# Scaling the attention probabilities on GpSimd in a two-layer hybrid decoder step

## Chip, cores and metric

One Trainium2 chip, one of its cores. The metric is the device time of the whole program in microseconds; a lower time is better. The kernel computes one inference step of two trunk layers for 512 prompt tokens with 16 learned tokens ahead of them, and for 8 sample tokens, with the same weights: 536 columns in all.

## The reference, cut to what matters

Each layer runs an attention over chosen keys, a gated linear recurrence, a merge of the two, and a feed-forward part. The change is in the prompt's attention: scores, softmax, and the product with the values.

```python
def attend_selected(q, k_sel, v_sel, valid):
    ...
    s = jnp.einsum('btngd,btknd->btngk', qg, k_sel.astype(jnp.float32)) * (HEAD_DIM ** -0.5)
    s = jnp.where(valid[:, :, None, None, :], s, -jnp.inf)
    p = jax.nn.softmax(s, axis=-1)
    o = jnp.einsum('btngk,btknd->btngd', p, v_sel.astype(jnp.float32))
    ...
def mixer_back(x, att, rec_o, gates, g_rec, w_pa_l, w_pb_l, w_o_l):
    ...
    a = att @ w_pa_l
    b = rec.reshape(B, T, REC_V) @ w_pb_l
    return x + (jax.nn.sigmoid(ga) * a + jax.nn.sigmoid(gb) * b) @ w_o_l
```

The softmax is over 528 keys or fewer for a tile of 128 queries. Its last step, dividing each row by its sum, is the operation that moves.

## The kernel before, in words

All orders of work are written out by hand, one instruction list for each engine, with semaphores between them. A layer has a front part (projections with the indexer and the top-k beside them), an **attention stage**, a merge, an output projection and the feed-forward part. Weights come in by DMA as tiles `raw`; ScalarE rounds each to a high part `w_hi` (`split`, L1426), GpSimd takes the remainder `w_lo` = `raw` - `w_hi` (`rest`, L667), and TensorE multiplies with both (L809). There are two buffers of `w_hi` and of `w_lo`, so the split of weight unit n waits until unit n-2 has been multiplied.

The attention stage has 17 blocks a layer (`BLK`), in the order (head pair 0: tiles 0, 1, 2, the short last tile of all heads, 3), then head pairs 1 to 3 with tiles 0 to 3. This text numbers them 0 to 16. A block has two halves s (two heads), and tile j has 128, 256, 384 or 512 key columns; block 3, the short tile, has 528. For each half of a block:

1. TensorE makes the scores in PSUM (`qk`, L1105), one block ahead.
2. VectorE adds the mask and takes the row's extremum, and writes `E` (`att_scores`, L2447); it waits also for the turns of the block before, since `E` is one buffer.
3. ScalarE takes the exponential of `E` in place, with the row's sum beside it (`att_exps`, L1695).
4. VectorE takes the reciprocal of both halves' sums in one instruction (L2456, semaphore `recips`).
5. ScalarE multiplies `E` by the reciprocal in place (`att_probs`, L1703, semaphore `probs`).
6. TensorE transposes `E` into PSUM (`turn`, L772), ScalarE copies it out as `pT` (L1709, L1712), TensorE multiplies it with the values (`pv`, L1137), and ScalarE copies the result out (L1609).

Between these steps stands the recurrence's work, put there by tables (`DVE_AHEAD`, `DVE_BEHIND`, `ACT_AHEAD`, `PE_AMID` and so on, with the block as key). On VectorE it is above all the steps `diff` (L2355, L2357) and `product` (L2364, L2366): `tensor_tensor` instructions with both inputs in SBUF, of 1024 or 1056 elements in each of 128 partitions. `DVE_BEHIND` is what stands right behind the reciprocal of a block:

```python
DVE_BEHIND = {..., 2: [("diff", 0, 1), ("diagonal", 1)],
              3: [("product", 0, 0), ("product", 0, 1)], 4: [("diff", 2, 0), ("scores", 0, 0)],
              5: [("product", 1, 0), ("product", 1, 1)], 6: [("product", 2, 0), ("product", 2, 1), ("scores", 1, 0)],
              7: [("diff", 4, 0), ("scores", 2, 0)], 8: [("product", 3, 0), ("product", 3, 1)],
              9: [("product", 4, 0), ("product", 4, 1), ("scores", 3, 0)], 10: [("diff", 6, 0), ("scores", 4, 0)],
              11: [("product", 5, 0), ("product", 5, 1)], 12: [("product", 6, 0), ("product", 6, 1), ("scores", 5, 0)],
              ..., 14: [("v_blk", 0)], ...}
```

`diagonal` and `scores` there are predicated copies out of PSUM (L2318, L2336), `v_blk` is a `tensor_tensor` of 8 partitions with both inputs in SBUF (L2387).

GpSimd clears two tensors ahead of the stage (L747, L750), takes the first two remainders of the merge's weights at its start, and then waits for the third, whose high part ScalarE makes behind the stage (`split_merge(2)`).

Of the kernel before, what the change touches and what calls it, by code (L numbers as in the profile page):

```python
# [76 lines left out]
def build(nc, t, out):  # L77
# [7 lines left out]
    ACT, ALU, AX = mybir.ActivationFunctionType, mybir.AluOpType, mybir.AxisListType  # L85
# [17 lines left out]
    WIDTH = [128, 256, 384, 512, 528]  # L103
# [7 lines left out]
    UA, UB, UC, UP, UO = 0, 16, 32, 48, 64  # L111
# [30 lines left out]
    BLOCKS = 17  # L142
# [9 lines left out]
    BLK = [(0, 0), (0, 1), (0, 2), (0, 4), (0, 3)] + [(n2, j) for n2 in range(1, 4) for j in range(4)]  # L152
# [44 lines left out]
    with ctx:  # L197
        def sb(name, shape, dt=f32):
            return ctx.enter_context(nc.sbuf_tensor(name, shape, dt))
# [52 lines left out]
        row_st = sb("row_st", [P, 2, 4])  # L252
# [7 lines left out]
        def place(name, shape, offset, dt=f32):  # L260

            n = 1
            for d in shape[1:]:
                n *= d
            n *= 1 if dt == u8 else 4
            assert offset + n <= size, (name, offset + n, size)
            return nc.alloc_sbuf_tensor_at(name, shape, dt, offset=base + offset)
# [30 lines left out]
        E = place("E", [P, 2, TP], o_ss)  # L298
# [93 lines left out]
        def wait(eng, name, L, per, n):  # L392

            eng.wait_ge(S[name], L * per + n)

        def hold(eng):

            eng.sem_inc(S["held"], 1)
# [27 lines left out]
        def turn_tile_of(s):  # L426

            return work[0][:, 512 * s:512 * s + 512]

        def last_turn(s):  # L430

            return acc[s][0:16, 1, 0:128]

        def short_turned(s):

            return pT[:, s, :, :].rearrange("p c t -> p (c t)")
# [53 lines left out]
        block = ctx.enter_context(nc.Block())  # L490
# [168 lines left out]
        def _(pool):  # L659
            pool.wait_ge(S["par_ready"], 1)  # L660
            for L in range(DEPTH):
                def rest(u, slot, kt):


                    s = slot % 2
                    pool.wait_ge(hi_done, L * UNITS + u + 5)  # L666
                    pool.tensor_tensor(w_lo[s][:, 0:kt, :], raw[slot][:, 0:kt, :], w_hi[s][:, 0:kt, :].bitcast(f32),  # L667
                                       ALU.subtract).then_inc(lo_done, 1)
# [79 lines left out]
                wait_unit(pool, L, UC + 15)  # L748
                hold(pool)
                pool.memset(Atail[:, :, :], 0.0).then_inc(S["scores_cleared"], 1)  # L750
                with pool.Fori(0, 4) as g:
                    for i in range(4):
                        rest(UP + g * 4 + i, i, 4)
                with pool.Fori(0, 2) as g:
# [628 lines left out]
        def _(act):  # L1383
# [26 lines left out]
            for L in range(DEPTH):  # L1410
# [115 lines left out]
                for j in range(1, 5):  # L1526
                    n = TILES[j][1]
                    for h in range(8):
# [3 lines left out]
                        w = min(512, WIDTH[j])  # L1532
# [165 lines left out]
                def att_probs(block):  # L1698

                    j, w = BLK[block][1], WIDTH[BLK[block][1]]  # L1700
                    for s in range(2):
                        wait(act, "recips", L, BLOCKS, block + 1)
                        act.activation(E[:, s, 0:w], E[:, s, 0:w], ACT.Copy, scale=row_st[:, s, 3:4])\  # L1703
                            .then_inc(S["probs"], 1)
                    for s in range(2):
                        act.wait_ge(turn_filled[s], L * BLOCKS + block + 1)
                        ps = turn_tile_of(s)
                        if j < 4:
                            act.activation(pT[:, s, 0:j + 1, :], ps[:, 0:(j + 1) * P].rearrange("p (c t) -> p c t", t=P),  # L1709
                                           ACT.Copy).then_inc(turn_drained[s], 1)  # L1710
                        else:
                            so(act.activation(short_turned(s)[:, 0:256].rearrange("p (m t) -> p m t", t=16),  # L1712
                                              ps.rearrange("p (m t) -> p m t", t=32)[:, :, 0:16], ACT.Copy))
                            act.activation(short_turned(s)[0:16, 256:320].rearrange("p (m t) -> p m t", t=16),
                                           last_turn(s).rearrange("p (m t) -> p m t", t=32)[:, :, 0:16],
                                           ACT.Copy).then_inc(turn_drained[s], 1)

                for block in range(STEPS):
                    if block < BLOCKS:
                        att_exps(block)  # L1720
                    if 0 < block <= BLOCKS:
                        att_drain(block - 1)
                    rec_steps(ACT_AHEAD.get(block, ()))
                    if block < BLOCKS:
                        att_probs(block)
                    rec_steps(ACT_BEHIND.get(block, ()))
# [874 lines left out]
```

## Time and profile before

| | |
|---|---|
| time, median of 3 runs | 2178.01 us (2175.06 to 2178.32) |
| the profiled execution's own time | 2177.8 us |
| its span in the trace | 2175.9 us |
| mean granted TensorE clock | 0.966 of full speed |
| busy TensorE, VectorE, ScalarE, GpSimd | 2009.2, 1210.8, 784.9, 760.8 us |
| attention stages, from the first `qk` to the first merge unit | 443.0 to 577.7 us and 1497.8 to 1635.2 us |

The span is measured from the first to the last instruction of the trace, and the time of the execution lies 1.9 us above it. Busy time is an average over all stages; in a stage it can be quite another engine that the rest waits for, so the stages are looked at one by one. A row of the timeline gives the start, the duration, engine, line, operation, output and inputs, and in brackets how long the engine had stood idle and for whom.

### The profile page before, as it was taken

How to read it: one execution, taken by the hardware profiler on the slowest of the kernel's cores; microseconds unless marked ns; L12 is line 12 of the kernel's file. 1: busy time of each engine (PE TensorE's matmuls, PEld its weight loads, DVE VectorE, ACT ScalarE, POOL GpSimd, SP SyncE). 2: the span in 40 equal slices, each digit the busy share in tenths (PEclk: the TensorE clock that was granted, in tenths of full speed). 3: DMA queues.
4: the chain of work that ended last, by engine and by line, in shares of the span. 5: the costliest groups of instructions: out<-in, count | busy, mean ns of one | idle time of the engine just before them, and what ended most of it. 6: DMA issues, size and time to landing. Idle time of an engine off the chain costs nothing. (4 is left out here: it accounts for less than half of the span.)

```text
span 2175.9 us, 40128 instructions
## 1 busy us (share of the span) xinstructions
PE 2009.2 (92%) x15610; PEld 1906.0 (88%) x15610; DVE 1210.8 (56%) x2159; ACT 784.9 (36%) x1217; POOL 760.8 (35%) x414
## 2 busy tenths in 40 slices
PE   3998999877989999999999899988888899999998
PEld 2987899866779999999999889987667899999998
DVE  3286777687465543045346677886754564412433
ACT  3243323267233343222323342225752334322233
POOL 1642338200034343443455223641001444434333
PEclk9999999899989999999999999998997999999999
DMA  5312236111332222332241323431033322223322
GB/s 132 110 59 78 59 93 184 57 39 46 93 113 88 87 87 77 97 90 83 82 144 52 88 59 88 152 114 48 2 99 104 98 87 87 80 85 97 91 69 82
DMA packets 309374, 189.18 MB, mean 87 GB/s; under 512 B 15904, under 2 KB 295552, under 8 KB 308224
## 3 DMA queue, kind: packets, MB, share of 16 engines
q1 hardware_dynamic: 299616, 160.51, 25.5%
q0 software_dynamic: 4224, 16.78, 2.2%
q10 hardware_dynamic: 5408, 10.16, 1.3%
q8 instruction: 85, 1.39, 0.3%
q14 instruction: 41, 0.34, 0.1%
HBM read 167.47 MB, written 18.10 MB: 85 GB/s over the span
## 5 line engine op out<-in xcount | busy, mean ns | idle before, releaser
L667 POOL TENSOR_TENSOR w_lo<-raw,w_hi 128x1024 fp32r<-128x1024 f32 (+3 forms) x290 | 630.0, 2174 | 1289.5 <-ACT w_hi L1426 1289.1
L809 PE MATMUL acc<-normed,w_hi 128*128 128x268 f32 x5696 | 964.0, 292 | 18.3 <-POOL w_lo L667 16.8
L809 PEld LDWEIGHTS acc<-normed,w_hi 128*128 128x128 f32 x5696 | 808.2, 191 | 41.5 <-issue 21.4
L1426 ACT ACTIVATE w_hi<-raw 128x1024 fp32r<-128x1024 f32 (+1 forms) x290 | 293.1, 1011 | 981.2 <-PE acc L809 952.7
L809 PE MATMUL acc<-normed,w_lo 128*128 128x268 f32 x2848 | 588.8, 289 | 0.0
L809 PEld LDWEIGHTS acc<-normed,w_lo 128*128 128x128 f32 x2848 | 449.5, 191 | 0.0
L809 PE MATMUL acc<-hidden,w_hi 128*128 128x268 f32 x1408 | 231.6, 287 | 0.0
L809 PEld LDWEIGHTS acc<-hidden,w_hi 128*128 128x128 f32 x1408 | 197.0, 189 | 0.0
L809 PE MATMUL acc<-hidden,w_lo 128*128 128x268 f32 x704 | 144.3, 287 | 0.0
L2544 DVE TENSOR_TENSOR hidden<-act_f,hidden 128x536 f32 x44 | 93.2, 2119 | 50.6 <-ACT hidden L1783 50.6
L2537 DVE TENSOR_TENSOR silu<-silu,rnorm 128x536 f32<-128x536 f32 x44 | 83.3, 1893 | 59.2 <-ACT silu L1780 59.2
L809 PEld LDWEIGHTS acc<-hidden,w_lo 128*128 128x128 f32 x704 | 109.8, 189 | 0.0
L809 PE MATMUL acc<-merged,w_hi 128*128 128x268 f32 x512 | 89.1, 299 | 9.5 <-POOL w_lo L667 9.5
L2519 DVE TENSOR_TENSOR x<-acc,x 128x536 f32<-128x536 f32 x32 | 22.9, 717 | 117.4 <-PE acc L809 117.4
L809 PEld LDWEIGHTS acc<-merged,w_hi 128*128 128x128 f32 x512 | 76.0, 200 | 10.3 <-POOL w_lo L667 5.4
L2554 DVE TENSOR_TENSOR x<-acc,x 128x536 f32 x16 | 11.5, 717 | 125.6 <-PE acc L809 125.6
L2534 DVE TENSOR_TENSOR silu<-acc,rnorm 128x536 f32<-128x536 f32 x44 | 31.5, 717 | 84.7 <-PE acc L809 84.0
L2540 DVE TENSOR_TENSOR act_f<-acc,silu 128x536 f32<-128x536 f32 x44 | 31.6, 717 | 80.2 <-PE acc L809 80.0
L1189 PE MATMUL work<-X 128*128 128x128 f32 x448 | 61.9, 297 | 9.2 <-issue 8.9
L1189 PEld LDWEIGHTS work<-X 128*128 128x128 f32 x448 | 57.8, 209 | 13.3 <-issue 13.2
L1416 ACT ACTIVATE relu<-work 128x256 f32<-128x256 f32 (+4 forms) x66 | 31.5, 502 | 86.0 <-PE work L948 68.1
L772 PEld LDWEIGHTS work<-cst,E 128*128 128x128 f32 x176 | 19.9, 147 | 41.4 <-issue 40.5
(334 smaller groups left out, 2846.1 us busy)
## 6 DMA issues: line engine op xcount, KB each, us to landing
raw<-in_w_in_dram SPq DMA_DIRECT2D x90, 512.0 KB, 3.7
raw<-in_w_gu_dram SPq DMA_DIRECT2D x88, 512.0 KB, 3.7
raw<-in_w_down_dram SPq DMA_DIRECT2D x32, 384.0 KB, 3.3
raw<-in_w_down_dram SPq DMA_DIRECT2D x32, 320.0 KB, 3.0
gate_scratch<-gate_out ACTq DMA_DIRECT2D x32, 268.0 KB, 3.0
normed<-gate_scratch SPq DMA_DIRECT2D x4, 2144.0 KB, 8.7
raw<-in_w_o_dram SPq DMA_DIRECT2D x16, 512.0 KB, 3.9
raw<-in_w_pa_dram SPq DMA_DIRECT2D x16, 256.0 KB, 6.3
```

The lines of the kernel that those rows point to most:

```text
L667: pool.tensor_tensor(w_lo[s][:, 0:kt, :], raw[slot][:, 0:kt, :], w_hi[s][:, 0:kt, :].bitcast(f32), ALU.subtract).then_inc(lo_done, 1)
L772: return pe.transpose(dst, src, ident[0:k, 0:k])
L809: mm = pe.matmul(acc[o][:, half, 0:HT], w[s][:, k, :], mov[:, part, k0 + k, half * HT:(half + 1) * HT], start=start and n == 0, stop=stop ...
L1189: mm = pe.matmul(ps[:, m * P:(m + 1) * P], at[:, h, c * P:(c + 1) * P], at[:, h, c * P:(c + 1) * P], start=True, stop=True)
L1416: act.activation(dst, ps if src is None else src, func, **kw).then_inc(drained[slot_of(item)], 1)
L1426: act.activation(w_hi[slot % 2][:, 0:kt, :], raw[slot][:, 0:kt, :], ACT.Copy).then_inc(hi_done, 1)
L2519: TT(halves(x[:, k, :]), acc[i][:, :, 0:HT], halves(x[:, k, :]), ALU.add).then_inc(taken[i], 1)
L2534: TT(halves(silu[:, :]), acc[0][:, :, 0:HT], halves(rnorm[:, :]), ALU.mult).then_inc(taken[0], 1)
L2537: TT(silu[:, :], silu[:, :], rnorm[:, :], ALU.mult).then_inc(S["up_scaled"], 1)
L2540: TT(halves(act_f[:, :]), acc[1][:, :, 0:HT], halves(silu[:, :]), ALU.mult).then_inc(taken[1], 1)
L2544: TT(hidden[:, 1, ds(g, 1), :].rearrange("p a t -> p (a t)"), act_f[:, :], hidden[:, 0, ds(g, 1), :].rearrange("p a t -> p (a t)").bitcast ...
L2554: TT(xk, acc[i][:, :, 0:HT], xk, ALU.add).then_inc(taken[i], 1)
```

## The change

In `att_probs` the two ScalarE multiplications of each block go. GpSimd does them instead, with `tensor_scalar` on the same `E` in place and the same reciprocal column, behind the same wait for `recips`, and it raises the same semaphore `probs`. So 34 instructions a layer move from ScalarE to GpSimd. GpSimd's loop over the merge's 16 remainders is opened for its first four: two before the 17 blocks, two behind them, and the other twelve in a loop as before. No DMA is added, removed or moved.

```diff
                 pool.memset(Atail[:, :, :], 0.0).then_inc(S["scores_cleared"], 1)
-                with pool.Fori(0, 4) as g:
+                for n in range(2):
+                    rest(UP + n, n, 4)
+                for block in range(BLOCKS):
+                    w = WIDTH[BLK[block][1]]
+                    wait(pool, "recips", L, BLOCKS, block + 1)
+                    for s in range(2):
+                        hold(pool)
+                        pool.tensor_scalar(E[:, s, 0:w], E[:, s, 0:w], row_st[:, s, 3:4], None, ALU.mult)\
+                            .then_inc(S["probs"], 1)
+                for n in range(2, 4):
+                    rest(UP + n, n, 4)
+                with pool.Fori(1, 4) as g:
                     for i in range(4):
                         rest(UP + g * 4 + i, i, 4)
...
                 def att_probs(block):

                     j, w = BLK[block][1], WIDTH[BLK[block][1]]
-                    for s in range(2):
-                        wait(act, "recips", L, BLOCKS, block + 1)
-                        act.activation(E[:, s, 0:w], E[:, s, 0:w], ACT.Copy, scale=row_st[:, s, 3:4])\
-                            .then_inc(S["probs"], 1)
```

GpSimd's list at the start of the attention stage of the first layer, before (`w_lo` is a remainder, `Asc` and `Atail` are score tensors of the recurrence):

```order
L747 MEMSET Asc 128x2048 [waits filled0]
L750 MEMSET Atail 16x64 [waits unit_done]
L751 UNCONDITIONAL_BRANCH
L751 ISA
L667 TENSOR_TENSOR w_lo<-raw,w_hi 128x512 [waits hi_done]
```

and now (lines behind the first edit count 11 more, behind the second one 7 more):

```order
L747 MEMSET Asc 128x2048 [waits filled0]
L750 MEMSET Atail 16x64 [waits unit_done]
L667 TENSOR_TENSOR w_lo<-raw,w_hi 128x512 [waits hi_done] x2
L758 ISA [waits recips]
L758 TENSOR_SCALAR E<-E,row_st 128x128 x2
L758 TENSOR_SCALAR E<-E,row_st 128x256 [waits recips]
L758 TENSOR_SCALAR E<-E,row_st 128x256
```

The multiplications stand in a plain row, and ahead of the first of the first layer stands an instruction of the kind ISA; the second layer's list has none there. In the built program it is a reload of GpSimd's instruction library, the same as the one that opens GpSimd's list, ahead of the first `w_lo` of the program.

ScalarE's list at blocks 5 and 6, before (`X` is the recurrence's operand, `proj_att` takes the attention's result):

```order
L1695 ACTIVATE E,row_st<-E,row_st 128x128 [waits qk_drained0]
L1695 ACTIVATE E,row_st<-E,row_st 128x128 [waits qk_drained1]
L1609 ACTIVATE proj_att<-work 128x128 [waits pv_filled]
L1624 ACTIVATE X_83<-X_83 128x4x16x16 [waits lev_diff]
L1703 ACTIVATE E<-E,row_st 128x128 [waits recips] x2
L1709 ACTIVATE pT<-work 128x128 [waits turn_filled0]
L1709 ACTIVATE pT<-work 128x128 [waits turn_filled1]
L1624 ACTIVATE X_83<-X_83 128x4x16x16 [waits lev_diff]
```

and now:

```order
L1706 ACTIVATE E,row_st<-E,row_st 128x128 [waits qk_drained0]
L1706 ACTIVATE E,row_st<-E,row_st 128x128 [waits qk_drained1]
L1620 ACTIVATE proj_att<-work 128x128 [waits pv_filled]
L1635 ACTIVATE X_83<-X_83 128x4x16x16 [waits lev_diff]
L1716 ACTIVATE pT<-work 128x128 [waits turn_filled0]
L1716 ACTIVATE pT<-work 128x128 [waits turn_filled1]
L1635 ACTIVATE X_83<-X_83 128x4x16x16 [waits lev_diff]
```

The pair of multiplications is out, and right behind it stands the copy that waits for TensorE's transposes of the same `E`. VectorE's list is as it was; in block 5 it reads, before and now but for the line numbers:

```order
L2357 TENSOR_TENSOR X_83<-proj_rec 128x4x16x16
L2456 RECIPROCAL row_st<-row_st 128x2 [waits exps]
L2364 TENSOR_TENSOR X_81<-X_81,proj_rec 128x4x8x32 [waits lev_exp]
L2366 TENSOR_TENSOR X_81<-X_81,K 128x4x8x32 [waits lev_exp]
L2447 ISA E,row_st<-acc,sc 128x256 [waits qk_filled0,turn_filled0]
```

Nothing moved here. Two products with both inputs in SBUF follow the reciprocal, and behind them the next block's scores, which wait for the turns of this one.

## Rows read from the trace of the kernel before

**Rows 1.** Busy time by stretch: both attention stages (us, engines' busy, PEclk, DMA, GB/s)

```profile
443.00:580.50 137.50, 113.08 (x934) 89.19 (x935) 95.89 (x218) 86.18 (x215) 1.14 (x1) 0.93 0.18 56
1497.80:1635.20 137.40, 112.33 (x922) 89.00 (x922) 95.32 (x215) 86.29 (x215) 1.34 (x2) 0.92 0.18 55
```

**Rows 2.** View of line L1703: who waited for it (us in all, times)

```profile
  PE work L772: 23.4, 14
```

**Rows 3.** Timeline of VectorE, second layer: behind the reciprocals of blocks 3 and 7

```profile
1517.07 0.17 DVE L2456 RECIPROCAL row_st<-row_st 128x2 f32<-128x2 f32 x1 [0.17 <-ACT E L1695]
1517.15 1.20 DVE L2364 TENSOR_TENSOR X<-X,proj_rec 128x1024 f32<-128x1024 f32 x1
1518.28 1.22 DVE L2366 TENSOR_TENSOR X<-X,K 128x1024 f32<-128x1024 f32 x1
...
1544.69 1.24 DVE L2355 TENSOR_TENSOR X<-proj_rec 128x1056 f32<-128x1056 f32 x1
1545.84 0.70 DVE L2336 COPY_PREDICATED Asc<-level_mask,work 128x512 f32<-128x512 uint8 x1
```

**Rows 4.** Timeline of ScalarE, second layer: the probabilities of blocks 3, 5, 6, 7

```profile
1518.05 1.35 ACT L1703 ACTIVATE E<-E,row_st 128x528 f32<-128x528 f32 x2
...
1533.60 0.69 ACT L1703 ACTIVATE E<-E,row_st 128x128 f32<-128x128 f32 x2
...
1537.70 0.91 ACT L1703 ACTIVATE E<-E,row_st 128x256 f32<-128x256 f32 x2
...
1544.81 1.12 ACT L1703 ACTIVATE E<-E,row_st 128x384 f32<-128x384 f32 x2 [1.21 <-DVE row_st L2456]
```

**Rows 5.** Timeline of TensorE, second layer: turns of blocks 2, 5, 6, 7, 12, 14

```profile
1513.11 1.02 PE L772 MATMUL work<-cst,E 128*128 128x128 f32 x6 [0.44 <-ACT E L1703]
...
1534.25 0.59 PE L772 MATMUL work<-cst,E 128*128 128x128 f32 x2 [1.18 <-ACT E L1703]
...
1538.68 0.66 PE L772 MATMUL work<-cst,E 128*128 128x128 f32 x4
...
1546.67 0.87 PE L772 MATMUL work<-cst,E 128*128 128x128 f32 x6
...
1579.12 1.94 PE L772 MATMUL work<-cst,E 128*128 128x128 f32 x8 [2.18 <-ACT E L1703]
...
1596.10 1.08 PE L772 MATMUL work<-cst,E 128*128 128x128 f32 x4 [3.35 <-ACT E L1703]
```

**Rows 6.** GpSimd: one remainder of 1024 columns (timeline), the clearing (groups by line)

```profile
1818.87 2.39 POOL L667 TENSOR_TENSOR w_lo<-raw,w_hi 128x1024 fp32r<-128x1024 f32 x1 [3.55 <-ACT w_hi L1426]
...
L747 POOL MEMSET Asc<- 128x2048 f32 x2 | 3.6, 1807 | 16.1 <-PE work L1048 16.1
```

**Rows 7.** VectorE by line (ns min/median/max), then timelines: GpSimd and VectorE around 1664 us

```profile
L2534 DVE TENSOR_TENSOR silu<-acc,rnorm x44: 716/717/717, 722.7 to 2096.8; 128x536 f32<-128x536 f32 x44
...
L2537 DVE TENSOR_TENSOR silu<-silu,rnorm x44: 717/2350/2362, 724.3 to 2098.6; 128x536 f32<-128x536 f32 x44
...
1662.22 1.28 POOL L667 TENSOR_TENSOR w_lo<-raw,w_hi 128x512 fp32r<-128x512 f32 x1 [14.68 <-ACT w_hi L1426]
1664.02 1.79 POOL L667 TENSOR_TENSOR w_lo<-raw,w_hi 128x512 fp32r<-128x512 f32 x1 [0.53 <-ACT w_hi L1426]
...
1662.38 1.69 DVE L2475 TENSOR_TENSOR proj_rec<-proj_rec 128x536 f32<-128x536 f32 x1 [11.08 <-ACT proj_rec L1656]
...
1663.99 2.40 DVE L2475 TENSOR_TENSOR proj_rec<-proj_rec 128x536 f32<-128x536 f32 x2
```

**Rows 8.** Views of lines L667 and L1426 (ns min/median/max): loads of code and tables

```profile
L667 POOLq MODIFY_POOL_CONFIG  x2: 11/11/11, 0.8 to 0.8; - x2
...
L1426 ACT ACT_TABLE_LOAD  x12: 1283/1283/1283, 718.9 to 1890.6; - x12
```

**Rows 9.** TensorE by stretch: behind the waits of blocks 5 and 12 (busy, PEclk)

```profile
1579.10:1583.00 3.90, 3.88 (x22) 0.59 0.00 0
1534.20:1537.80 3.60, 2.96 (x22) 1.00 0.00 0
```

## The prediction

> **What bounds the kernel now.** I read four views: the stretches of busy time, the view of the line that moves, the timelines of three engines in the second layer's attention stage, and, for prices that the stage doesn't show, the views of GpSimd's and VectorE's lines elsewhere. Only the two attention stages, of 137 us each, are concerned, and in neither is one engine full: TensorE is busy 113 us, VectorE 95, ScalarE 86, GpSimd one [rows 1]. So a loop of waits sets their length: scores, exponential, reciprocal, probabilities, turns, and then the scores of the next block, which VectorE may not write into `E` before this block's turns. TensorE waits for the probabilities 14 times, 23.4 us in all [rows 2], seven blocks a layer (2, 3, 5, 8, 11, 12, 14). There the reader can see the loop bite: what the probabilities lose, TensorE and the next block lose too. In the other blocks TensorE comes to the turns later, from work of its own, and that is cover: in block 6 the pair ends at 1538.61 and the turns start at 1538.68, in block 7 at 1545.93 and 1546.67, so 0.07 and 0.74 us of it [rows 4, 5].
>
> **What leaves.** 68 ScalarE multiplications. A pair takes 0.69, 0.91 and 1.12 us at 128, 256 and 384 columns and 1.35 at 528 (taken for 512 too) [rows 4], and starts about 0.05 us behind the reciprocal: 0.74, 0.96, 1.17 and 1.40 us from the reciprocal to the second half's end. In block 3 it stood behind another ScalarE instruction: the reciprocal ends at 1517.24, the pair at 19.40, so 2.16 us [rows 3, 4]. Block 12 has the same pattern and is taken alike. ScalarE gains no more by this than the queueing in those two blocks, since the next thing on its list is the copy of `pT`, which waits for the turns and so for the same probabilities.
>
> **What comes: the price of one GpSimd multiplication, h.** The trace has none. The nearest rows bound it. Clearing 2048 columns, which only writes, takes 1.807 us, 0.88 ns a column: h is no less. A remainder, which reads two inputs and writes one, takes 2.39 us for 1024 columns and 1.28 for 512 when nothing disturbs it [rows 6, 7]: 0.17 us and 2.17 ns a column, and h is no more. One input read and one output written lies between the two, so I take the middle: 0.28, 0.48, 0.67, 0.87 and 0.89 us for 128, 256, 384, 512 and 528 columns. The Trainium skill (GPSIMD Engine Reference, Engine selection) says that GpSimd runs one-input operations at roughly line rate; by its 1.2 GHz (Specifications) that is an estimate of 0.43 us for 512 columns, and the sum would be the low end below.
>
> **What comes: the wait for VectorE.** With one input in PSUM, VectorE's instruction of 536 columns takes 717 ns in all 44 cases; with both in SBUF the same shape has a median of 2350 [rows 7]. The rows around 1664 us show why: GpSimd's remainder runs to 1663.50 and VectorE's first product, started at 1662.38, ends only at 1664.07, 0.57 behind it. The next remainder, begun at 1664.02 beside VectorE's second product, takes 1.79 us in place of 1.28, and then the third product ends at 1666.39, 0.58 behind that remainder. Each waits for the whole of what the other is at, and they take turns. In the attention stage VectorE issues just such an instruction right behind the reciprocal, before GpSimd can have seen it, in blocks 2 to 12 and 14. The Trainium skill (SBUF — State Buffer, Who interferes with whom) gives this as a rule for any GpSimd instruction that reads SBUF, one input or two. No row here has a GpSimd instruction with one input beside VectorE: by the rule the sum below stands, and without it the second rival's does.
>
> So, from the reciprocal's end: VectorE's first product leaves the port after 1.04 us (1517.24 to 1518.28), GpSimd's first half takes h, VectorE's second product, which has waited, 1.13 (1517.15 to 1518.28), GpSimd's second half h, and the hand-over to TensorE some 0.1 [rows 3]. Where two products follow (blocks 3, 5, 6, 8, 9, 11, 12) that is 2.27 + 2h; where one does and then a predicated copy out of PSUM, as in block 7 [rows 3] (2, 4, 7, 10, 14), 1.14 + 2h.
>
> **The sum for a layer**, new time less old time less cover, in us:
> - block 2 (384 columns): 2.48 - 1.17 = 1.31
> - block 3 (528): 4.05 - 2.16 = 1.89
> - block 5 (128): 2.83 - 0.74 = 2.09
> - block 8 (512): 4.01 - 1.40 = 2.61
> - block 11 (384): 3.61 - 1.17 = 2.44
> - block 12 (512): 4.01 - 2.16 = 1.85
> - block 14 (256): 2.10 - 0.96 = 1.14
> - block 6 (256): 3.23 - 0.96 - 0.07 = 2.20
> - block 7 (384): 2.48 - 1.17 - 0.74 = 0.57, and block 4 (512), with the same cover: 0.74
> - blocks 0, 1, 9, 10, 13, 15, 16: TensorE doesn't wait there [rows 2], and behind the reciprocals of 13, 15 and 16 no such product stands; nothing. The cover is TensorE's own work, and if it is gone blocks 9 and 10 cost up to 2.1 and 1.1 more.
>
> 16.8 us a layer, **33.7** for both. With the low price of h the same lines give 10.4 a layer and 20.7, with the high one 23.6 and 47.2. That VectorE's products end later by h is in this: the loop runs through the probabilities, and the next scores wait for the turns anyway.
>
> **Smaller terms.** TensorE's clock: behind block 5's wait of 1.18 us it is granted in full (2.4 GHz), behind block 12's of 2.18 us at 0.59, most of it at the lower level of 1.2 GHz [rows 5, 9]. With the terms above the waits of blocks 5, 6 and 11 also pass 2 us. A stretch such as block 12's, 3.9 us at 0.59, holds 2.3 us of work at the full clock, so 1.6 us are lost; half may lie beside other waits, so 3 x 2 x 0.8, some 4 us, between 0 and 10. The reload of GpSimd's library, which the order shows once, behind the first wait for a reciprocal, with TensorE about to need the result: the row of the same instruction shows 11 ns twice and then an idle engine, so nothing above is excluded; the nearest row of an engine that loads what it needs is ScalarE's table load, 1.28 us [rows 8], which I take, between 0.02 and some 10. The Trainium skill (GPSIMD Engine Reference, Instruction dispatch) states about 6 us for the first call after a load; with it the sum is 5 us higher. The opened loop and the two remainders behind the blocks cost nothing: ScalarE makes their high parts only behind its own attention loop, so GpSimd is idle there before and after; were GpSimd still at a block, the merge's third unit would wait for it. SP's queue is untouched.
>
> 33.7 + 4 + 1.3 = 39 us on 2177.8 of the profiled execution, which is within 0.2 us of the median of the runs: **2217 us**.
>
> **The rivals.**
> 1. *Waits slow TensorE throughout.* If each of the eight blocks with a term over 1.1 us lost a whole 1.6 us to the clock, that is 8 x 2 x 1.6 = 26 in place of 4: 2239 us. For it: block 14's turns, behind a wait of 3.35 us, take 1.08 us for 4 matmuls where block 6's take 0.66 [rows 5]. Against it: block 5's wait leaves the clock full, and three blocks a layer pay it already.
> 2. *Not slower: GpSimd's one-input multiplication does not exclude VectorE's products.* Then a block takes 0.18 + 2h, which meets ScalarE's time at the middle h (128 columns: 0.74 against 0.74), and decides by h alone: the change pays below ScalarE's own rate. In the blocks named above, with the reload: at the middle h about 1.1 us a layer, 2181 us; at the low one -3.7 a layer (blocks 3 and 12 alone -1.1 each, since the pair no longer queues), 2172; at the high one 7 a layer, 2193. For it: no row has such an instruction. Against it: the remainders show that a reading GpSimd instruction excludes VectorE, and a second input is no obvious condition for that.
>
> **How the numbers follow.** Forecast 0.78, with its own range from 2198 (20.7 and no smaller terms) to 2239 (47.2 + 10 + 4). First rival 0.08. Second 0.14, spread over 2172 to 2193: faster, same and slower about alike. About 0.2%, 4.4 us, is what a measurement here can tell from no change. Faster 0.05, same 0.05, slower 0.78 + 0.08 + 0.04 = 0.90. The range of 2190 to 2242 takes in the forecast's and the first rival's, and the top of the second's.
>
> **What would show each step right or wrong.** In the profile after: GpSimd's 68 `tensor_scalar`, alone at 0.3 to 0.9 us by width, and about 1 us longer where they run into a product; VectorE's products behind reciprocals at 1.6 to 2.1 us in place of 1.2; TensorE's waits for the probabilities at some 55 us in place of 23, with GpSimd as releaser; both attention stages some 17 to 20 us longer, and the rest of the program as it was. Products that stay at 1.2 us beside GpSimd would make the second rival right. A gap at the first GpSimd multiplication of the first layer alone is the reload. A stage longer by much more than its waits for probabilities would be the clock.

## The result: 65 us slower, above the range

| | before | changed |
|---|---|---|
| time, median | 2178.16 us | 2242.90 us (2241.87 to 2243.07) |
| ratio, 95% interval | | 1.0295 (1.0277 to 1.0313) |
| span of the profiled execution | 2175.9 us | 2241.3 us |
| mean granted TensorE clock | 0.966 | 0.949 |
| attention stages, first `qk` to first merge unit | 134.9 and 137.4 us | 168.3 and 168.5 us |

The forecast was 2217 us in a range of 2190 to 2242. The sign and the place were right: both stages grew, by 64.5 us together, and the rest of the program by 0.9. The size was forecast at 39 us and came out at 64.7.

Both attention stages by stretch (columns: us, busy PE, PEld, DVE, ACT, POOL, granted clock, DMA share, GB/s). The first line is the first stage of the kernel before, since its line in [rows 1] runs 2.8 us into the merge; the second stage stands there as it is:

```profile
442.86:577.74 134.88, 110.46 (x922) 86.58 (x922) 94.88 (x215) 86.32 (x215) 1.28 (x2) 0.94 0.19 57
...
443.56:611.89 168.33, 125.80 (x923) 97.66 (x923) 97.04 (x214) 69.68 (x181) 56.52 (x35) 0.83 0.15 45
1532.31:1700.77 168.46, 125.69 (x922) 97.59 (x922) 97.12 (x214) 69.79 (x181) 56.70 (x35) 0.83 0.15 46
```

ScalarE lost 16 us of work a layer, GpSimd took 55 on, VectorE's time is nearly the same. TensorE is busy 15 and 13 us longer with the same number of multiplications, at a granted clock of 0.83 in place of 0.94 and 0.92.

The view of the line that came in, and who waited for it, against [rows 2]:

```profile
L758 POOL TENSOR_SCALAR E<-E,row_st x68: 596/1558/3472, 447.9 to 1676.3; 128x128 f32<-128x128 f32 x16, 128x256 f32<-128x256 f32 x16, 128x384 f32<-128x384 f32 x16, 128x512 f32<-128x512 f32 x16
L758 POOLq MODIFY_POOL_CONFIG  x2: 10/10/10, 447.8 to 447.8; - x2
...
  PE work L783: 64.0, 40
```

TensorE waits 64.0 us for probabilities, 40 times, in place of 23.4 us, 14 times. The reload takes 10 ns, and the first multiplication starts at 447.9, behind it.

GpSimd's pairs of the second layer: blocks 0, 1, 3, 7, 13, 15 and 16:

```profile
1536.64 1.66 POOL L758 TENSOR_SCALAR E<-E,row_st 128x128 f32<-128x128 f32 x2 [3.15 <-DVE row_st L2463]
1541.64 2.29 POOL L758 TENSOR_SCALAR E<-E,row_st 128x256 f32<-128x256 f32 x2 [3.34 <-DVE row_st L2463]
1557.29 5.02 POOL L758 TENSOR_SCALAR E<-E,row_st 128x528 f32<-128x528 f32 x2 [4.08 <-DVE row_st L2463]
1594.44 3.28 POOL L758 TENSOR_SCALAR E<-E,row_st 128x384 f32<-128x384 f32 x2 [4.74 <-DVE row_st L2463]
1648.71 1.18 POOL L758 TENSOR_SCALAR E<-E,row_st 128x128 f32<-128x128 f32 x2 [6.43 <-DVE row_st L2463]
1665.83 2.46 POOL L758 TENSOR_SCALAR E<-E,row_st 128x384 f32<-128x384 f32 x2 [4.00 <-DVE row_st L2463]
1674.75 3.10 POOL L758 TENSOR_SCALAR E<-E,row_st 128x512 f32<-128x512 f32 x2 [6.45 <-DVE row_st L2463]
```

Behind the reciprocals of blocks 13, 15 and 16 no product follows at once, so half of these pairs is the price: h = 0.59, 1.23 and 1.55 us. The first half of block 3, alone in the timeline, takes 3.44 us, which leaves 1.58 for the second; in the same way block 14's second half has 0.90. So h is **0.60, 0.90, 1.24, 1.56 and 1.58 us** at 128, 256, 384, 512 and 528 columns. The prediction had 0.28 to 0.89, with 1.31 as its upper end.

VectorE's two products behind block 3's reciprocal, against [rows 3]:

```profile
1557.00 1.20 DVE L2371 TENSOR_TENSOR X<-X,proj_rec 128x1024 f32<-128x1024 f32 x1
1558.12 1.22 DVE L2373 TENSOR_TENSOR X<-X,K 128x1024 f32<-128x1024 f32 x1
```

They are as long as before, one right behind the other. GpSimd's first half was issued during the first, and ended at 1560.73: 1.39 us behind the second. It waited for both, and its second half waited for none.

TensorE's turns of blocks 0, 3 (both halves) and 5, and the multiplications behind block 0, against [rows 5]:

```profile
1537.97 1.04 PE L783 MATMUL work<-cst,E 128*128 128x128 f32 x2 [0.62 <-POOL E L758]
1540.36 3.75 PE L1190 MATMUL work<-proj_rec,K 128*128 128x128 f32 x16 [0.25 <-issue]
...
1560.99 1.09 PE L783 MATMUL work<-cst,E 128*128 128x128 f32 x4 [4.44 <-POOL E L758]
1562.56 1.09 PE L783 MATMUL work<-cst,E 128*128 128x128 f32 x4 [0.28 <-POOL E L758]
...
1582.38 0.30 PE L783 MATMUL work<-cst,E 128*128 128x128 f32 x1 [3.31 <-POOL E L758]
```

The waits of blocks 3 and 5 were 2.03 and 1.18 us. Block 0 had none. In the kernel before, its turns and the 16 multiplications behind them read

```profile
1502.95 0.63 PE L772 MATMUL work<-cst,E 128*128 128x128 f32 x2
...
1504.94 2.02 PE L1179 MATMUL work<-proj_rec,K 128*128 128x128 f32 x16 [0.50 <-issue]
```

Behind a wait of only 0.62 us the same 16 now take 3.75.

### The profile page after: what moved, and what is told of

Same layout as the page of the kernel before. It is cut to its first block and busy times, and to the rows that moved or that the text cites. A ratio compares the mean times of both kernels' runs of the same rounds, so it can differ in the third digit from the quotient of the medians.

```text
span 2241.3 us, 40186 instructions
## 1 busy us (share of the span) xinstructions
PE 2038.0 (91%) x15610; PEld 1925.9 (86%) x15610; DVE 1215.0 (54%) x2159; ACT 752.1 (34%) x1149; POOL 871.4 (39%) x482
## 3 DMA queue, kind: packets, MB, share of 16 engines
q8 instruction: 85, 1.39, 0.3%
## 5 line engine op out<-in xcount | busy, mean ns | idle before, releaser
L667 POOL TENSOR_TENSOR w_lo<-raw,w_hi 128x1024 fp32r<-128x1024 f32 (+3 forms) x290 | 629.6, 2172 | 1066.6 <-ACT w_hi L1437 1066.3
L758 POOL TENSOR_SCALAR E<-E,row_st 128x128 f32<-128x128 f32 (+4 forms) x68 | 111.0, 1641 | 177.7 <-DVE row_st L2463 177.7
L783 PE MATMUL work<-cst,E 128*128 128x128 f32 x176 | 38.7, 342 | 64.6 <-POOL E L758 64.0
L1200 PE MATMUL work<-X 128*128 128x128 f32 x448 | 70.1, 322 | 5.2 <-issue 5.2
```

Of the source, the lines that this page charges most:

```text
L758: pool.tensor_scalar(E[:, s, 0:w], E[:, s, 0:w], row_st[:, s, 3:4], None, ALU.mult)\
L783: return pe.transpose(dst, src, ident[0:k, 0:k])
L1200: mm = pe.matmul(ps[:, m * P:(m + 1) * P], at[:, h, c * P:(c + 1) * P], at[:, h, c * P:(c + 1) * P], start=True, stop=True)
```

## Experiments

Three questions were open. How much of the 64.7 us is the lower clock, how much the price h, how much the wait for VectorE? Why is h so high, and why did VectorE's products stay as they were? And can a kernel keep what the change gains without what it costs?

### 1. TensorE kept busy through the waits

```diff
+    FILL = {0: 2, 2: 11, 3: 30, 5: 22, 8: 33, 11: 27, 12: 14, 14: 32}
...
+                    if s == 0:
+                        for _ in range(FILL.get(block, 0)):
+                            transpose(ps[:, 0:P], ident)
                     wait(pe, "probs", L, 2 * BLOCKS, 2 * block + s + 1)
```

The multiplications of the identity are issued as transposes of it.

> The changed kernel, with multiplications of the identity put on TensorE ahead of the wait for the probabilities of blocks 0, 2, 3, 5, 8, 11, 12 and 14: 2, 11, 30, 22, 33, 27, 14 and 32 of them, so many as fill the wait that the changed kernel shows there, less 0.3 us, at the full clock. Their result is overwritten. Theory A (the waits cost twice: once as waits, 40.6 us more than before, and again as a lower granted clock behind them, TensorE being busy 29 us longer in the two stages): the clock of the stages rises from 0.83 to above 0.93, the busy time without the added work falls from 126 to some 113 us a stage, and the time to about 2217 us (2210 to 2228). Rival B (the slower TensorE lies beside other waits, so the clock is a by-product): the clock rises and the time stays at 2243.

Measured: 2236.17 us, ratio to the kernel before 1.0250 (1.0225 to 1.0275). The stages, the added work included, and three rows of TensorE (block 0's followers, block 3's filling and turns):

```profile
443.64:608.46 164.82, 135.50 (x1093) 109.08 (x1094) 96.97 (x214) 69.93 (x181) 58.75 (x35) 0.92 0.15 47
1529.06:1693.94 164.88, 135.48 (x1094) 109.11 (x1094) 96.95 (x214) 69.93 (x181) 58.82 (x35) 0.92 0.15 47
```

```profile
1536.96 2.02 PE L1194 MATMUL work<-proj_rec,K 128*128 128x128 f32 x16 [0.50 <-issue]
...
1552.08 3.46 PE L784 MATMUL work<-cst 128*128 128x128 f32 x30 [0.65 <-ACT proj_att L1624]
1555.77 0.63 PE L784 MATMUL work<-cst,E 128*128 128x128 f32 x4 [0.22 <-POOL E L759]
```

The filling always ended before the probabilities came (0.22 us here), and the clock came back to 0.92. The eight fillings of a layer take 20.5 us, so the work proper fell from 125.7 to 115 us a stage. Yet a stage is only 3.5 us shorter: TensorE, faster, waits longer for the same probabilities. Theory A expected 13 a stage and falls; rival B, none, is nearer. **The clock costs 7 us** here by the stages (by the ratios, 1.0295 less 1.0250, it is some 10 us, give or take 7). Some 2 of each 3.5 lie in block 0: from the stage's start to block 1's turns it is 13.09 us in the changed kernel (1532.31 to 1545.40), 10.84 here and 9.89 before.

### 2 and 3. A scaled identity

The change of width alone, on GpSimd:

```diff
-                        pool.tensor_scalar(E[:, s, 0:w], E[:, s, 0:w], row_st[:, s, 3:4], None, ALU.mult)\
+                        pool.tensor_scalar(scaled_ident[:, s, :], C("ident"), row_st[:, s, 3:4], None, ALU.mult)\
...
-                        mm = transpose(at, E[:, s, c * P:c * P + w])
+                        mm = pe.matmul(at, E[:, s, c * P:c * P + w], scaled_ident[:, s, :], start=True, stop=True)
```

> The changed kernel, but GpSimd multiplies the identity by the reciprocal, 128 columns in every block, and TensorE's transposes are multiplications of E with that scaled identity. GpSimd's instruction, its engine, its waits and its place are those of the changed kernel; its width alone is smaller, so h is 0.60 us in every block in place of 0.60 to 1.58. Theory A (port wait and price h add up on the loop): the pairs take 1.2 us alone, 3.0 where two of VectorE's products follow the reciprocal, 2.0 where one does; TensorE's waits fall by 10 to 11 us a layer, and the time to 2210 to 2222. Rival C (it is the port alone that costs): 2240 or more. Rival D (it is the price alone): 2178 to 2190.

The same on VectorE, from the kernel before (ScalarE's pair goes too):

```diff
                         vec.reciprocal(row_st[:, :, 3], row_st[:, :, 2]).then_inc(S["recips"], 1)
+                        wait(vec, "recips", L, BLOCKS, block + 1)
+                        TT(scaled_ident, C("ident").unsqueeze(1).broadcast_to((P, 2, P)),
+                           row_st[:, :, 3:4].broadcast_to((P, 2, P)), ALU.mult).then_inc(S["probs"], 2)
```

> The kernel before, with no multiplication of E at all: VectorE multiplies the identity by both halves' reciprocals, one instruction of 2 x 128 columns right behind the reciprocal, and TensorE multiplies E with the scaled identity in place of transposing it. From the reciprocal's end to TensorE's start some 0.5 us in every block, in place of 0.74 to 1.40 (2.16 in blocks 3 and 12). If the loop through the probabilities bounds the stage (as theory A says), TensorE's waits for them fall from 23 us to some 12 and the time to 2164 to 2174. Rival E (VectorE has 17 more instructions of some 0.4 us a layer, and they delay the products and scores behind them): 2176 to 2186. A matmul with the scaled identity that takes longer than the transpose would show in TensorE's busy time.

Measured: 2240.70 us, 1.0271 (1.0244 to 1.0297), and 2195.02 us, 1.0057 (1.0035 to 1.0080). GpSimd's pair of block 3 in the first, and TensorE's line in each:

```profile
1556.32 3.02 POOL L759 TENSOR_SCALAR pT<-cst,row_st 128x128 f32<-128x128 f32 x2 [4.59 <-DVE row_st L2464]
```

```profile
L1133 PE MATMUL work<-pT,E x352: 275/275/582, 448.2 to 1681.6; 128*128 128x128 f32 x176
```

```profile
L1122 PE MATMUL work<-pT,E x352: 273/275/580, 450.3 to 1641.6; 128*128 128x128 f32 x176
```

In the first the pairs are as expected (3.02 of 3.0), and TensorE's waits for the probabilities fell from 64.0 us to 46.1, 9 a layer. But the multiplication by the scaled identity runs as 352 instructions of 275 ns where the transposes were 176. TensorE's busy time in the two stages rose by 22 us against the changed kernel and by 26 against the kernel before. Neither time lies where theory A put it; the first lies where rival C did and the second above both of its ranges. Both are inconclusive on h: what the probabilities gained, the turns, which stand in the same loop, gave back.

### 4. Other forms of the instruction

```diff
-                        pool.tensor_scalar(E[:, s, 0:w], E[:, s, 0:w], row_st[:, s, 3:4], None, ALU.mult)\
+                        if s == 0:
+                            pool.tensor_tensor(E[:, s, 0:w], E[:, s, 0:w],
+                                               row_st[:, s, 3:4].broadcast_to((P, w)), ALU.mult).then_inc(S["probs"], 1)
+                        else:
+                            pool.tensor_scalar(E[:, s, 0:w], E[:, s, 0:w], 1.0, None, ALU.mult).then_inc(S["probs"], 1)
```

> The changed kernel with two other forms of GpSimd's instruction: the first half of each block as a two-input multiplication by the broadcast reciprocal, the second half as a multiplication by the constant 1 (so the second half is left without its scaling). Prices are read where nothing disturbs GpSimd (blocks 13, 15, 16). If the price lies in the form with a scalar read from memory, the constant one costs about half of 1.56 us at 512 columns and the two-input one 1.28, as the remainder does; if it is the price of any such instruction, all three cost 1.3 to 1.6. On the port: if a two-input instruction gets it between VectorE's two products, as a remainder did at 1664 us of the kernel before, the first halves of blocks 3, 5, 6, 8, 9, 11 and 12 take 0.8 us more than their price, and the second product 1.2 us longer; if a waiting GpSimd gets the port only when VectorE pauses, 1.9 us more, and the products stay at 1.2.

Measured: 2220.07 us in one run. GpSimd's two halves of block 3 and of block 16, and VectorE's products behind block 3's reciprocal:

```profile
1544.23 1.86 POOL L759 TENSOR_TENSOR E<-E,row_st 128x528 f32<-128x528 f32 x1 [4.06 <-DVE row_st L2466]
1546.07 2.50 POOL L762 TENSOR_SCALAR E<-E 128x528 f32<-128x528 f32 x1
...
1656.52 1.04 POOL L759 TENSOR_TENSOR E<-E,row_st 128x512 f32<-128x512 f32 x1 [7.80 <-DVE row_st L2466]
1657.53 1.49 POOL L762 TENSOR_SCALAR E<-E 128x512 f32<-128x512 f32 x1
```

```profile
1543.96 1.20 DVE L2374 TENSOR_TENSOR X<-X,proj_rec 128x1024 f32<-128x1024 f32 x1
1545.09 2.09 DVE L2376 TENSOR_TENSOR X<-X,K 128x1024 f32<-128x1024 f32 x1
```

At 512 columns: two inputs 1.04 us, one input and a constant 1.49, one input and a scalar from memory 1.56. So it is not the number of inputs that makes the price, and reading the scalar adds only 0.07; neither of the two answers expected fits. On the port the two-input form does what the prediction had said of the change: it gets in between VectorE's two products, 0.8 us above its price, and the second product is 2.09 us in place of 1.22 (0.87 longer, where 1.2 was expected).

### 5 and 6. The two forms, each in both halves

The first has the two-input line of experiment 4 in both halves, the second its line with the constant in both.

> The changed kernel with GpSimd's multiplication written as a two-input instruction, E times the reciprocal column broadcast over the columns, in both halves. Its price alone is 0.40, 0.61, 0.83 and 1.04 us (the last run's rows), against 0.60, 0.90, 1.24 and 1.56 of the changed kernel. Theory A (what is lost is, block by block, the wait for VectorE's products plus two prices, worked out as in the prediction with measured prices): by the prediction's own lines 19.9 us a layer in place of 28.1, so the attention stages are 155 to 158 us long in place of 168 and the time 2209 to 2222 us. VectorE's second product behind a reciprocal is longer by GpSimd's price, 1.6 to 2.2 us in place of 1.2, and the first halves take 0.85 us more than their price, as do the second ones. Rival F (the price makes no difference, since the reach of the wait for VectorE sets the pace): over 2235.

> The changed kernel with GpSimd's scalar a constant 1 in place of the reciprocal column, in both halves; so the scaling of the probabilities is left out. All else is as in the changed kernel: the same operation, waits and places. Its price alone is 0.53, 0.85, 1.17 and 1.49 us, 0.07 less. Theory G (reading the scalar from memory is an access of its own: it gets the port between VectorE's two products, and the multiplication then has to wait again): without it the first halves in blocks 3, 5, 6, 8, 9, 11 and 12 take 0.85 us more than their price in place of 1.9, and VectorE's second product is longer by that price, to 1.7 to 2.6 us; the time falls by more than the price, to 2225 to 2238. Rival H (it is the operation itself that loses the port to the next instruction of VectorE): first halves 1.9 us above their price, products at 1.2, time 2238 to 2243.

Measured: 2209.17 us, 1.0167 (1.0115 to 1.0220), with stages of 155.7 and 155.6; and 2221.12 us, 1.0222 (1.0157 to 1.0288). Of the two-input kernel the first half of block 3 and all second products:

```profile
1535.77 1.87 POOL L758 TENSOR_TENSOR E<-E,row_st 128x528 f32<-128x528 f32 x1 [4.06 <-DVE row_st L2463]
```

```profile
L2373 DVE TENSOR_TENSOR X<-X,K x14: 1423/1884/2097, 464.8 to 1610.3; 128x1056 f32<-128x1056 f32 x8, 128x1024 f32<-128x1024 f32 x6
```

Of the kernel with the constant the same half and the product beside it:

```profile
1547.01 2.32 POOL L758 TENSOR_SCALAR E<-E 128x528 f32<-128x528 f32 x1 [4.07 <-DVE row_st L2463]
```

```profile
1547.86 1.64 DVE L2373 TENSOR_TENSOR X<-X,K 128x1024 f32<-128x1024 f32 x1
```

The two-input kernel bears theory A out: the prediction's own lines give 39.8 us for its prices, and its stages are 39.0 longer than before. Up to block 1's turns it loses only 0.2 us a layer. With the constant the first half is 0.81 us above its price in place of 1.86, as theory G says. So it is the read of the scalar that makes the multiplication wait for VectorE's second product as well. The product is longer by 0.42 us, though, where G expected the whole price of 1.5: this form and VectorE's product run beside each other for most of the time, and the kernel is 4 us below what G expected at best.

### 7 and 8. VectorE's products cut short

```diff
+                    if few:
+                        xv, qv, kv = xv[:, 0:1, 0:1, :], qv[:, 0:1, 0:1, :], kv[:, 0:1, 0:1, :]
```

`few` is set for the products behind the reciprocals; in the first run on the changed kernel, in the second on the kernel before.

> The changed kernel with VectorE's products behind the reciprocals of blocks 3, 5, 6, 8, 9, 11 and 12 cut to one head and one group of columns (64 columns or fewer of 1024), so that most of the recurrence's products are left out. GpSimd's pairs there then take twice their price: 1.2, 1.8, 2.5, 3.1 us, in place of 3.0 to 5.0. Theory A: the wait for VectorE (2.05 us of a block's term) goes from six blocks with a term, 12 us a layer; the time falls to 2205 to 2222, and what then stays above the kernel before (some 30 to 40 us) is the price. Rival D (it is the price alone): 2235 to 2243. Rival C (it is the port alone): 2178 to 2190.

> The kernel before with the same products cut to one head and one group of columns, as the control of the run ahead of it: what the missing work of VectorE is worth where ScalarE scales the probabilities. The products lie beside the probabilities and the turns there, so the time should stay at 2170 to 2180. If it falls by more than 8 us, the products were on the path of the kernel before too, and the run ahead of it has to be read against this one.

Measured: 2214.66 us, 1.0193 (1.0136 to 1.0250), and 2176.55 us, 1.0011 (0.9983 to 1.0039). GpSimd's pair of block 3 in the first:

```profile
1543.27 3.18 POOL L758 TENSOR_SCALAR E<-E,row_st 128x528 f32<-128x528 f32 x2 [4.08 <-DVE row_st L2465]
```

It is twice the price. The control stays where the kernel before is, so in sum the products themselves cost nothing there. In the control's trace the two stages are longer than before by 11 us, though, and the rest of the program is shorter by 8, as it is in the other kernel's; so the split that follows is good to some us only. The difference of the two, 38 us, is the price with what is left of the clock and of the waits behind single products; the other 27 of the 64.7 are the wait for the paired products. Theory A holds, rivals C and D fall.

### 9. Only the seven blocks that were set at nothing

```diff
+    ON_POOL = (0, 1, 9, 10, 13, 15, 16)
...
-                for block in range(BLOCKS):
+                for block in ON_POOL:
...
-                    for s in range(2):
+                    for s in range(0 if block in ON_POOL else 2):
```

> The change in seven of the 17 blocks alone: GpSimd scales the probabilities of blocks 0, 1, 9, 10, 13, 15 and 16, the ones that the prediction's sum sets at nothing, and ScalarE those of the other ten, as before. Theory A (the sum's lines of nothing hold, since TensorE comes later to those turns): the changed kernel shows two waits of some 0.5 us there (blocks 0 and 10), so 2178 to 2182 us, within 0.2% of the kernel before. Rival I (these blocks lose too, because the copies, scores and exponentials behind their turns come later): 2185 or more, that is 4 us a layer and up.

Measured: 2188.13 us, 1.0036 (1.0019 to 1.0054), 8 us more: rival I by the time, but in the second layer not by its mechanism. TensorE in blocks 0 and 1 of the second layer, and two stretches with their granted clock (seventh column after the stretch), the second one of the kernel before:

```profile
1512.08 1.03 PE L784 MATMUL work<-cst,E 128*128 128x128 f32 x2 [0.66 <-POOL E L759]
...
1514.47 3.75 PE L1191 MATMUL work<-proj_rec,K 128*128 128x128 f32 x16 [0.25 <-issue]
1519.53 0.66 PE L784 MATMUL work<-cst,E 128*128 128x128 f32 x4
```

```profile
1512.08:1518.20 6.12, 5.32 (x24) 4.19 (x24) 3.90 (x15) 2.63 (x9) 2.62 (x3) 0.50 0.42 126
```

```profile
1502.95:1508.40 5.45, 4.53 (x31) 3.01 (x30) 5.16 (x19) 3.67 (x12) 0.00 (x0) 0.93 0.59 177
```

From the stage's start to block 1's turns it is 13.08 us (1506.45 to 1519.53), against 9.89 before, and that loss of 3.2 is in sum the whole of this layer's 3.3 (stages 140.69 and 137.38 us). Block 0's turns come 0.5 us later, behind a wait of 0.66, and then TensorE works at 0.50, the level of 1.2 GHz, where it had 0.93.

The wait is not needed for that fall. In the control of experiment 8 nothing is changed ahead of block 3, ScalarE scales block 0, and TensorE doesn't wait for it; yet the same 16 multiplications take 3.75 us in both layers. In the second one:

```profile
1505.69 0.63 PE L772 MATMUL work<-cst,E 128*128 128x128 f32 x2
...
1507.68 3.75 PE L1179 MATMUL work<-proj_rec,K 128*128 128x128 f32 x16 [0.25 <-issue]
```

Block 1's turns come 2.0 us later there than in the kernel before. So this place can fall to the lower level without GpSimd. The changed kernel falls in both layers and filling its wait prevents it; what else tips it is open.

In the first layer 2.6 us are lost in the same place, and 5.4 more later. Of these, 2.6 lie between the turns of blocks 3 and 4, which ScalarE scales: behind block 3's turns the granted clock is 0.55, against 0.82 in the second layer. Another 1.8 lie in blocks 9 and 10, for which TensorE waits 0.80 and 0.17 us in this kernel. The second layer hides that loss, since the kernel before is itself 1.6 us slower between the turns of blocks 8 and 9 there than in its first layer.

### 10 to 12. What the change gains, without its cost

```diff
+    FILL = {2: 1, 3: 12, 5: 6, 8: 12, 11: 7, 12: 8, 14: 22}
...
-    ACT_AHEAD = {3: [("exp", 0, 1)], 4: [("exp", 1, 0)], 5: [("exp", 2, 0)], 6: ["last_decay"], 8: [("exp", 4, 0)],
-                 11: [("exp", 6, 0)], 12: [("key_exp", 1)], 13: [("key_exp", 4)], 15: [("rec_out", 0)],
+    ACT_AMID = {3: [("exp", 0, 1)]}
+    ACT_AHEAD = {4: [("exp", 1, 0)], 5: [("exp", 2, 0)], 6: ["last_decay"], 8: [("exp", 4, 0)],
+                 11: [("exp", 6, 0)], 13: [("key_exp", 4)], 15: [("rec_out", 0)],
...
-                  10: [("exp", 5, 1)], 11: [("exp", 6, 1), ("key_exp", 0)], 12: [("key_exp", 2), ("key_exp", 3)],
+                  10: [("exp", 5, 1)], 11: [("exp", 6, 1), ("key_exp", 0)], 12: [("key_exp", 1), ("key_exp", 2), ("key_exp", 3)],
```

`FILL` is used as in experiment 1, on the kernel before; `ACT_AMID` stands between ScalarE's multiplications and its copies.

> The kernel before, ScalarE scaling all probabilities, but with nothing queued ahead of them in blocks 3 and 12: the exponential of level 0's second half moves from ahead of block 3's multiplications to right behind them, the exponentials of the keys' second tile from ahead of block 12's to behind its copies; and multiplications of the identity (1, 12, 6, 12, 7, 8 and 22 of them in blocks 2, 3, 5, 8, 11, 12 and 14) fill most of TensorE's waits for the probabilities. This takes the one gain of the change, that the pair no longer queues, without GpSimd's price. By the first profile the probabilities come 0.95 us earlier in block 3 and 1.2 in block 12, of which 0.4 to 1 reaches the loop: 2 to 4 us for both layers; the filling is worth a share of what it gave in the changed kernel (7 us on 64 us of waits, so 2 to 3 us on 23). Expected 2171 to 2176, ratio 0.997 to 0.999. If the displaced steps are late for VectorE's products or the next exponentials instead: 2178 to 2184.

> One half of the last run of the kernel before: only the multiplications of the identity that fill TensorE's waits for the probabilities; ScalarE's steps stand where they stood. The clock behind the waits of blocks 3, 8, 12 and 14 (0.59 in block 12) should be granted in full. If the clock gave the 6 to 8 us of that run, this one gives most of it: 2171 to 2174 where the kernel before has 2178 to 2180. If the moved steps gave it, 2176 to 2180.

> The other half: only the two steps of ScalarE that stood ahead of the probabilities of blocks 3 and 12 are moved behind them; nothing is filled. If the queueing in those blocks gave the gain, 2172 to 2176; if the clock did, 2177 to 2181.

Measured: both 2172.21 us, ratio 0.9970 (0.9957 to 0.9984); the filling alone 2174.15, 0.9971 (0.9955 to 0.9987); the moved steps alone 2177.65, 0.9984 (0.9970 to 0.9999). The stages with the filling alone:

```profile
442.83:577.43 134.60, 117.37 (x991) 92.25 (x991) 95.09 (x215) 86.31 (x215) 1.29 (x2) 0.95 0.19 58
1497.69:1632.25 134.56, 117.38 (x990) 92.22 (x990) 95.06 (x215) 86.27 (x215) 1.24 (x2) 0.95 0.19 58
```

Against the trace of the kernel before the first stage gains 0.3 us and the second 2.8; the traces are of one execution each. So **the kernel before with its waits filled beats both the kernel before and the changed one**, the former by some 0.3%. The moved steps add nothing that can be told apart from it; alone they are at the edge of what can be measured.

## Why the prediction was wrong in size

- **The loop of waits as the bound: right.** The probabilities' delay is most of what the stages grew by, and VectorE's and ScalarE's spare time bought nothing. With VectorE's products cut, the kernel before keeps its time in sum (experiment 8).
- **The price h: the step that failed.** "One input read and one output written lies between the two" did not hold: the instruction is dearer than the two-input remainder that was to bound it from above, 1.56 us against 1.28 at 512 columns. The Trainium skill (GPSIMD Engine Reference, Engine selection) pointed the other way still, with an estimate of 0.43 us; the trace has 3.6 times as much. Put the measured h into the prediction's lines and nothing else: 2.45, 3.27, 2.73, 3.99, 3.58, 3.23, 1.98, 3.04, 1.71 and 2.12 us for blocks 2, 3, 5, 8, 11, 12, 14, 6, 7 and 4, which is 28.1 a layer and **56.2** in place of 33.7. Why the one-input form is the dearer one, no run shows.
- **The lines block by block, with the measured h: eight of the ten right within 0.45 us.** This takes a block's cost as the growth, in the second layer, from the turns of the second half of the block ahead to its own. Block 4 grew by 3.06 us for 2.12, and block 7 by nothing for 1.71. Behind block 6's turns TensorE had stood idle for 1.33 us, for a reason that the trace doesn't name, and now it doesn't; so block 7 had more cover than the 0.74. The ten together grew by 25.4 and 25.6 us in the two layers, where the lines give 28.1. The work behind block 6's turns, before and now:

```profile
1540.67 2.02 PE L1189 MATMUL work<-X 128*128 128x128 f32 x16 [1.33 <-issue]
...
1590.20 1.95 PE L1200 MATMUL work<-X 128*128 128x128 f32 x16
```

- **The wait for VectorE: right in size, wrong in how.** The pairs are 1.86 us above 2h in block 3 and 0.80 in block 7, with 0.2 from the reciprocal's end to their start and 0.25 from their end to TensorE's turns: 2.31 and 1.25 for 2.27 and 1.14. But GpSimd and VectorE don't take turns here: GpSimd waits for both products and VectorE for nothing, so its products stayed at 1.2 us where 1.6 to 2.1 were forecast. For the second half, which ends the pair, that is the same. So the sign that was to speak for the second rival came true, products at 1.2 us, without that rival being right: it doesn't tell a GpSimd that VectorE leaves alone from one that waits for it. The Trainium skill (SBUF — State Buffer, Who interferes with whom) has it that "Issue order, not op shape, decides who blocks"; here the shape does decide, since at the same place of the list the two-input form gets in before the second product and the change's form behind it.
- **The clock: 7 us against 4, inside its bounds of 0 to 10, but mostly elsewhere.** It was put behind blocks 5, 6 and 11; some 4 of the 7 lie in block 0, set at nothing for want of a wait. That the size came out near is luck, all the more as this place falls to the lower level in the control too (experiment 9). The first rival's sign came true in the records (0.83, and 29 us more of TensorE's busy time on the page), its price did not: a busy TensorE that would wait anyway costs nothing.
- **The blocks at nothing: wrong.** Blocks 0 and 1 cost 3.2 us a layer, most of it this clock. GpSimd's pairs there are 0.46 and 0.49 us above twice the price, beside VectorE's scans (L2316, two inputs in SBUF), which the prediction's list of blocks leaves out. From block 9 on, the blocks at nothing and the end of the stage cost 2.5 us in the second layer and 4.6 in the first; how much of that lies in the clock of the one trace of the kernel before is open.
- **The reload, 1.3 us: nothing.** Its rows are 10 ns, and the first pair of the first layer takes 1.58 us where the second layer's has 1.66. The Trainium skill (GPSIMD Engine Reference, Instruction dispatch) states some 6 us; no run here shows it.
- **The second rival** (no exclusion by a one-input instruction) is not what happened, but the form with a constant comes near to it.

In the trace the growth of 64.5 us is 51.0 in the ten blocks with a term, 6.4 in blocks 0 and 1, and 7.1 in the rest. The sum of 56.2 + 6.4 + the 3 that filling gave elsewhere, some 65 us, agrees with the 64.7 measured by luck: 5 us too much in the ten blocks stand against 4 too little in the rest.

## What to carry to other kernels

Price an operation on GpSimd from a row of that very form; a row of another form need not bound it: here the row that was to lie above lay below. For a column of scalars, a two-input multiplication with the column broadcast was a third cheaper here and got to memory sooner. Before a lower TensorE clock is counted as a loss, see whether TensorE waits for something anyway: filled waits cost nothing and gave 0.3% on the kernel before, where 9 us of filling a layer took the place of idle time.

## What the runs showed of the hardware

- GpSimd, 128 x 512 in fp32, undisturbed: 1.04 us with two inputs (one a broadcast column), 1.49 with one input and a constant, 1.56 with one input and a scalar from memory; 0.40, 0.53 and 0.60 at 128 columns. The two-input form has no reload of the library ahead of it.
- Against two VectorE products in a row, each with two SBUF inputs, GpSimd's first half was 0.8 us above its price with two inputs (second product 1.4 to 2.1 us), 0.8 with a constant (second product 1.3 to 1.7), 1.9 with a scalar from memory (second product 1.2).
- A wait of 0.62 us was followed by 16 multiplications at the level of 1.2 GHz, 3.75 us for 2.02; two transposes of the identity in that wait brought the 2.02 back. In the control of experiment 8 the same 16 took 3.75 us with no wait ahead of block 0's turns, at a granted clock of 0.50 from there to their end.
- A transpose as a multiplication by a scaled identity runs as two instructions of 275 ns each where the transpose is one.
